# Third expert's down weights requested without waiting for the first gather

## The reference, cut to what matters

```
for layer in range(2):
    x = x + mixer(rmsnorm(x, norm_mix_w[layer]), w_in[layer], ..., w_out[layer])
    x = x + hierarchical_moe(rmsnorm(x, norm_ffn_w[layer]), ...)
return rmsnorm(x, norm_final_w)

# in hierarchical_moe
eid = g_idx * 8 + top_k(expert logits within the group, 2)   # two experts per token
a = silu(xblk @ w_expert_gate[e]) * (xblk @ w_expert_up[e])  # 1024 -> 512
y = a @ w_expert_down[e]                                     # 512 -> 1024
out = segment_sum(y * weight, token)
```

## Time and profile before

| | us |
|---|---|
| Median of three runs | 1559.06 |
| Profiled execution, its own time | 1559.34 |
| Its span in the trace | 1556.1 |
| PE busy | 1468.9 (94%) |
| DVE busy | 801.9 (52%) |
| ACT busy | 336.6 (22%) |
| POOL busy | 269.0 (17%) |
| Bytes moved by DMA | 464.03 MB, mean 298 GB/s |

### The profile page before, as it was taken

The page is one execution under the profiler, slowest core; times in us unless marked ns, Lnnn a source line. Parts: engine busy times, 40 slices in busy tenths (PEclk is TensorE's granted clock), DMA queues, the critical chain, the costliest instruction groups (busy, mean ns, idle before and its releaser), DMA issues.

```text
span 1556.1 us, 19195 instructions
## 1 busy us (share of the span) xinstructions
PE 1468.9 (94%) x7242; PEld 780.8 (50%) x7242; DVE 801.9 (52%) x1457; ACT 336.6 (22%) x642; POOL 269.0 (17%) x156
## 2 busy tenths in 40 slices
PE   7999999799999999989899999996999999998996
PEld 5877768633333333333378777684433333333332
DVE  4047764545555555444541586635455555544445
ACT  4335562100000000000252454710000000000002
POOL 4433332100000000000134332401000000000001
PEclk9999999799999999999999999997999999999998
DMA  6432144799999999999733321449999999999995
GB/s 191 116 94 68 41 162 176 288 396 419 418 419 420 419 418 419 420 418 420 297 109 95 82 68 28 162 192 352 419 419 420 419 418 419 419 420 419 419 420 207
DMA packets 124460, 464.03 MB, mean 298 GB/s; under 512 B 18995, under 2 KB 62131, under 8 KB 74961
## 3 DMA queue, kind: packets, MB, share of 16 engines
q1 hardware_dynamic: 116752, 449.13, 72.9%
q0 software_dynamic: 6272, 12.60, 2.2%
q10 hardware_dynamic: 1344, 1.05, 0.2%
HBM read 464.84 MB, written 6.29 MB: 303 GB/s over the span
## 4 chain that ended last, share of the span: by engine, by line
PE 65%; SPq 24%; DMA 4%; DVE 4%; issue 2%; ACT 1%; DVEq 0%; POOLq 0%; ACTq 0%
SPq L567 20%; PE bank L1649 16%; PE bank L1664 8%; PE bank L1501 5%; PE bank L1626 5%; PE bank L1503 5%; PE bank L1502 5%; SPq L577 4%; DMA area<-in_w_expert_up_dram 4%; PE bank L1568 2%; PE bank L1570 2%; PE bank L1569 2%; PE bank L1484 2%; PE bank L1486 2%; PE bank L1485 2%
## 5 line engine op out<-in xcount | busy, mean ns | idle before, releaser
L1649 PE MATMUL bank<-area 128*64 128x512 f32 x2048 | 462.1, 601 | 25.7 <-DMA area<-in_w_expert_up_dram 24.1
L1335 DVE TENSOR_TENSOR xres<-xres,bank 128x512 f32<-128x512 f32 x512 | 316.5, 680 | 1.9 <-PE bank L1626 1.8
L1649 PEld LDWEIGHTS bank<-area 128*64 128x64 f32 x2048 | 140.9, 138 | 314.8 <-issue 270.5
L1664 PE MATMUL bank<-area 128*64 128x512 f32 x1024 | 233.8, 598 | 6.9 <-DVE area L1342 2.1
L711 POOL DMA_INDIRECT area<-rows,gath x64 | 72.2, 1128 | 752.2 <-PE bank L1618 720.6
L1316 DVE TENSOR_TENSOR area<-area,bank 128x256 f32<-128x256 f32 x64 | 27.0, 421 | 327.6 <-ACT area L951 327.6
L685 POOL TENSOR_TENSOR w_lo<-area,w_hi 128x1024 fp32r<-128x1024 f32 x58 | 142.7, 2462 | 294.4 <-ACT w_hi L784 294.4
L951 ACT ACTIVATE area<-bank 128x256 f32<-128x256 f32 x64 | 24.6, 385 | 531.7 <-PE bank L1649 531.7
L1501 PE MATMUL bank<-h_hi,w_hi 128*128 128x512 f32 x336 | 135.1, 402 | 2.2 <-DVE h_lo L1162 2.1
L1664 PEld LDWEIGHTS bank<-area 128*64 128x64 f32 x1024 | 67.9, 136 | 131.7 <-issue 109.6
L1503 PE MATMUL bank<-h_hi,w_lo 128*128 128x512 f32 x336 | 131.2, 390 | 0.0
(11 more groups left out here) (174 smaller groups left out, 1634.7 us busy)
## 6 DMA issues: line engine op xcount, KB each, us to landing
area<-in_w_expert_up_dram SPq DMA_DIRECT2D x128, 1024.0 KB, 26.6
area<-in_w_expert_gate_dram SPq DMA_DIRECT2D x128, 1024.0 KB, 24.7
area<-in_w_expert_down_dram SPq DMA_DIRECT2D x64, 2048.0 KB, 28.4
area<-in_w_in_dram SPq DMA_DIRECT2D x58, 512.0 KB, 3.9
area<-in_w_out_dram SPq DMA_DIRECT2D x4, 2048.0 KB, 10.5
rows<-area POOLq DMA_DIRECT2D x8, 512.0 KB, 6.3
area<-in_decay_dram SPq DMA_DIRECT2D x2, 1024.0 KB, 5.8
out_dram<-area SPq DMA_DIRECT2D x4, 512.0 KB, 2.9
```

Source lines behind the costliest of these rows:

```text
L1335: tt(xs, xs, bank[4 + i][:, :], ALU.add).then_inc(s_sa[i], 1)
L1649: last = mm(bank[1][SLOTS * half:SLOTS * (half + 1), :], xT[:, c % 4, c // 4, :], w[:, :, c, 256 * half:256 * (half + 1)], start=(c == 0), ...
L1664: last = mm(bank[3][SLOTS * half:SLOTS * (half + 1), :], hx[:, c % 2, c // 2, :], w[:, c, 512 * half:512 * (half + 1)], start=(c == 0), st ...
```

## The change

The wait of SP for the first gather is taken out. Expert 2's down weights are then issued directly behind expert 2's up weights. Nothing else changes. It is in the loop over layers, so it acts twice.

```
                 for half in range(2):
                     load_rows(layer, 2, 2, half, 1)
 
-
-                sp.wait_ge(s_gat[0], 16 * (layer * len(range(0, NE, 3)) + 1))
                 load_down(layer, 2, 2)
```

## The result

The changed kernel's median is 1568.7 us against 1559.13 us for the kernel before, five runs each. One of the five runs of the changed kernel was far slower (2479 us) and is left out of what follows; the median of the other four is 1567.7 us. Their ratio to the kernel before is 1.0052, with a 95% interval of 1.0040 to 1.0063: 8.1 us slower, 6.2 to 9.8 us, which puts the changed kernel at 1567.2 us. The forecast was 1566.0 us, from 7.0 us of loss, with a range of 1561.0 to 1569.5 us. The profiled execution took 1566.77 us, with a span of 1564.7 us; that span is 8.6 us longer than before. Lines of the kernel after have numbers lower by 2 from the change on, so L1647 is the L1649 of before.

A forecast was written before the change was run, and what follows sets the result against it. The full weight stream from expert 3's first piece, which waits on PE and the first gather, was taken to bound each layer. 2 x 3.5 = 7.0 us on 1559.34, less 0.3 for the median: 1566.0 us, range 1561.0 to 1569.5.

The forecast's parts named there:

- The wait was not on the path: SP's wait for the first gather, 32.9 us in two waits: removing it by itself is worth nothing.
- The 2 MB lay in a hole: Expert 2's down load, 309 to 315 us: moving its 5.0 us gains 0, at most 0.5 us a layer.
- The queue stays full 5.0 us longer, to 310.3 and 1079 us: SP's load queue around the first gather: 2 MB more keep it full 5.0 us longer in each layer.
- A gather in full engines takes 7.0 us, a delay of 3.5 us: First gather of each layer, sharing the engines with the added load: 7.0 us instead of 3.23, taken as 3.5 us late.
- the first term: The first gather's delay in full engines, 3.5 us a layer, 2 x 3.5 = 7.0 us in all.
- Nothing covers it, and the stream keeps the loss: From gather to layer end: transposition, gate and up, expert 3's first piece and the full stream all move by 3.5 us.
- The clock gives nothing back: PE's clock rise in expert 0's gate and up moves with the delayed work: 0, up to 1 us either way a layer.
- The gather not held up: First gather: its descriptors get a turn at once, or expert-stage gathers are slow for another reason; 1559.1 us, chance 0.14.
- The clock that gives half back: Expert 0's gate and up: the clock rises at its old time, giving back 1.75 us a layer; 1562.6 us, chance 0.09.
- The stream that gains: At 309 to 317 us: expert 3's stream starts earlier, by at most 5.0 us a layer; 1549.1 us, chance 0.04.
- The gather behind everything: First gather stands behind all the added bytes, 5.0 us a layer; 1569.1 us, chance 0.05.

## Why the prediction was right

**The wait was not on the path.** Right. Taking it away and giving its place to another load changes nothing (ratio 1.0000).

**The 2 MB lay in a hole.** Right for layer 0, and only there worked out. In layer 1 the bytes of the down load ended when expert 3's first piece was issued. I had no row of layer 1 for that place, and used layer 0's for both. That it did no harm was luck: the change moves the bytes forward. In the run where they move back I forecast a loss of 4.2 us, and it was 7.5 us.

**The queue stays full 5.0 us longer, to 310.3 and 1079 us.** Right as a length: it emptied at about 312 and 1085 us, in an execution that was 0.9 us and 5.3 us late at these places. That is 0.8 and 0.7 us more than said. I had not added the gathers' own bytes, 0.45 MB on q0 from 304 to 313 us, which are about 1 us at 419 GB/s by estimate.

**A gather in full engines takes 7.0 us, a delay of 3.5 us.** Right: 6.92 and 6.85 us, 3.69 and 3.54 us late. I had taken a little off because the queue would empty before the landing; it did not, and that is the 0.2 us in the first term. The picture behind the number was not quite right: I wrote that the gather shares the engines over its whole flight, but it has no packet in them for its first 4.2 us. In full engines the whole delay was between 3.5 us here and 4.8 us where the load was issued just before the gather. Of it, the wait up to the gather's first packet took 2.4 to 2.8 us (from 1.8 us to between 4.2 and 4.6 us); the rest was lost afterwards, while the packets of both queues moved side by side.

**Nothing covers it, and the stream keeps the loss.** Right: first piece 5.0 us later in layer 0, of which 0.9 us are from before, and 8.8 us later in layer 1 and 8.6 us at the end. The stretch at 419 GB/s has no gaps.

**The clock gives nothing back.** Right, within 0.3 us. The rise moved with the work, in layer 0 to about 319.3 us, 5.5 us after gate and up started (4.8 before), in layer 1 to about 1090.7 us, 3.8 us after (3.9 before). The traces give the clock as 0.50 and 1.00 of full speed, and no run shows the values in GHz that I put beside it. In stretches of 1 us, columns as above:

```profile
319.00:320.00 1.00, 1.00 (x6) 0.38 (x4) 0.93 (x4) 0.00 (x0) 0.00 (x0) 0.84 0.00 0
...
1090.00:1091.00 1.00, 1.00 (x6) 0.26 (x4) 0.90 (x4) 0.00 (x0) 0.00 (x0) 0.64 0.02 8
```

**The rivals.** The gather not held up: refuted by all runs with the load ahead. The clock that gives half back: refuted. The stream that gains: refuted in both layers, for expert 3's first piece is issued 4.0 and 3.5 us later after the gather's start than before, and nothing comes back behind it. The gather behind everything: it gave 1569.1 us. The ratio's 1567.2 us is nearer to my 1566.0, but the interval reaches to 1568.9 us, and the time alone could hardly have told the two apart. The run with more ahead of the gather refutes it.

What stays open: the intervals allow 6.2 to 9.8 us, the shown terms are 7.2 us, or 7.5 us with the clock. I can't say whether the rest is more than the scatter of the runs, whose profiles start up to 0.9 us apart before the changed line, one of them with 1.7 us a layer more by the clock of the last expert. And what decides that the gather's first packet waits 4.2 us in full engines, no run shows.

## What to carry to other kernels

A wait in a load queue can be worth its time for what it keeps off the DMA engines, here 8.1 us in two layers. Before taking one away, ask which small transfer on the path flies at that moment, and read its price in full engines from a later stage of the same trace (6.7 to 7.2 us there, 6.92 and 6.85 us here). And where a stream of weights bounds a stage, find the moment from which it is full, in every layer by itself: here bytes moved in front of that moment cost the stream nothing, although they cost the gather that they met; bytes moved behind it cost about their transfer time less what was left of the hole (in layer 0 2.6 us, for 2 MB of 5.0 us; the 4.3 us of layer 1 are explained in part only); and what delayed the moment was not made up later in any run.

## What was unexpected of the hardware

The price of the bulk load to the gather is a step: 7.6 us when it was issued 0.4 us after the gather's start, 3.8 us at 1.0 us. A load issued from 0.2 us before to 0.4 us after the gather's start cost it at least as much (7.3 to 8.1 us) as a queue that had long been full (6.9 to 7.3 us). In both cases no packet of the gather moved for 4.2 to 4.6 us, against 1.8 us otherwise. And matmuls issued to hold PE's clock up did not hold it: the granted clock fell to 0.50 in both layers, at 304.9 and 1072.9 us, and was back at 1.00 for gate and up in the first only (7.09 us against 9.89).
